# Projecting the values of four heads in one block, tokens stationary, in a two-block float32 kernel on one Trainium2 core

## What is computed

```
z_f, z_b, i, q, g = split(h @ w_in)              # w_in: 2048 x 10240; q and g for x alone
v = heads(i)                                     # 16 heads of 128
for each direction (forward, backward), each head:
    f = lb + (1 - lb) * sigmoid(z);  k = (1 - lb) * sigmoid(-z)
    b = cumsum(log f) in chunks of 64 tokens
    dS[n] = (k * exp(b_last - b))[n].T @ v[n];  S[n+1] = exp(b_last) * S[n] + dS[n]
    scores = mask((q * exp(b)) @ (k * exp(-b)).T)
    o += (q * exp(b)) @ S[n] + scores @ v
y = rms(o) * onorm_g * silu(g) @ w_out
```

## Time and profile before

| | us |
|---|---|
| median of 3 runs | 2552.0 (2551.85 to 2552.26) |
| the profiled execution | 2551.78 |
| its span | 2550.0 |
| PE busy | 2505.7 (98%) |
| DVE busy | 1648.3 (65%) |
| ACT busy | 1125.4 (44%) |

### The profile page before, as it was taken

How to read it: one execution, slowest core, us unless ns; L and a number is a source line. 1 busy time by engine, 2 the same in 40 slices (tenths; PEclk the granted TensorE clock), 3 DMA queues, 4 the chain that set the end, 5 groups by cost and what they waited for, 6 DMA issues and landing times.

```text
span 2550.0 us, 34782 instructions
## 1 busy us (share of the span) xinstructions
PE 2505.7 (98%) x13215; PEld 2059.8 (81%) x13215; DVE 1648.3 (65%) x2404; ACT 1125.4 (44%) x1923; POOL 0.2 (0%) x4
## 2 busy tenths in 40 slices
PE   6999999999999999999999999999999999999998
PEld 2578788888887888888888888878888887987887
DVE  2368789788997546464545557567566757657664
ACT  3422122222225635353534446456455646555563
POOL 0000000000000000000000000000000000000000
PEclk8999999999999999999999999999999999999999
DMA  9975376656675523333332425665544465644463
GB/s 372 375 272 171 119 214 190 201 168 214 229 247 165 151 81 103 94 99 99 94 104 82 115 83 180 203 221 176 176 154 157 162 238 183 189 159 154 165 212 134
DMA packets 380893, 440.34 MB, mean 173 GB/s; under 512 B 23086, under 2 KB 254312, under 8 KB 378856
## 3 DMA queue, kind: packets, MB, share of 16 engines
q1 hardware_dynamic: 372544, 414.24, 50.3%
q10 hardware_dynamic: 8232, 24.52, 2.6%
HBM read 430.29 MB, written 8.41 MB: 172 GB/s over the span
## 4 chain that ended last, share of the span: by engine, by line
PE 94%; DVE 2%; DMA 2%; ACT 1%; issue 1%; ACTq 0%; DVEq 0%; SPq 0%
PE ps L1280 15%; PE ps L1281 15%; PE ps L1282 15%; PE ps L1283 13%; PE ps L1285 13%; PE ps L1284 13%; PE ps L1304 1%; DMA raw<-in_ada_w_dram 1%; PE ps L1957 1%; PE ps L1965 1%; PE ps L1660 1%; PE ps L1652 1%; PE ps L1689 1%; PE ps L1664 1%; PE ps L1418 1%
## 5 line engine op out<-in xcount | busy, mean ns | idle before, releaser
L2058 DVE TENSOR_TENSOR wl<-raw,wh 128x1024 fp32r<-128x1024 f32 (+1 forms) x586 | 693.6, 1206 | 316.9 <-ACT wh L665 308.7
L665 ACT ACTIVATE wh<-raw 128x1024 fp32r<-128x1024 f32 (+1 forms) x586 | 596.6, 1043 | 624.4 <-PE ps L1285 237.7
L1280 PE MATMUL ps<-hTh,wh 128*128 128x512 f32 (+1 forms) x1820 | 681.4, 374 | 3.4 <-DVE wl L2058 1.9
L1281 PE MATMUL ps<-hTl,wh 128*128 128x512 f32 (+1 forms) x1820 | 673.8, 370 | 0.0
L1282 PE MATMUL ps<-hTh,wl 128*128 128x512 f32 (+1 forms) x1820 | 672.1, 369 | 0.0
L1283 PE MATMUL ps<-wh,hTh 128*128 128x512 f32 (+2 forms) x1568 | 614.9, 392 | 2.3 <-DVE hTl L2778 2.3
L1285 PE MATMUL ps<-wh,hTl 128*128 128x512 f32 (+2 forms) x1568 | 604.7, 386 | 0.0
L1284 PE MATMUL ps<-wl,hTh 128*128 128x512 f32 (+2 forms) x1568 | 603.7, 385 | 0.0
L1280 PEld LDWEIGHTS ps<-hTh,wh 128*128 128x128 f32 x1820 | 342.8, 188 | 71.6 <-issue 7.5
L1282 PEld LDWEIGHTS ps<-hTh,wl 128*128 128x128 f32 x1820 | 342.2, 188 | 60.0
L1281 PEld LDWEIGHTS ps<-hTl,wh 128*128 128x128 f32 x1820 | 343.0, 188 | 58.7 <-issue 1.0
(11 more groups left out here) (310 smaller groups left out, 1869.9 us busy)
## 6 DMA issues: line engine op xcount, KB each, us to landing
raw<-in_ada_w_dram SPq DMA_DIRECT2D x96, 1024.0 KB, 5.9
raw<-in_w_in_dram SPq DMA_DIRECT2D x88, 1024.0 KB, 5.2
raw<-in_od_w_in_dram SPq DMA_DIRECT2D x256, 256.0 KB, 3.8
raw<-in_ev_w_in_dram SPq DMA_DIRECT2D x192, 256.0 KB, 4.3
raw<-in_w_out_dram SPq DMA_DIRECT2D x32, 1024.0 KB, 5.1
raw<-in_ev_w_out_dram SPq DMA_DIRECT2D x16, 1024.0 KB, 5.1
raw<-in_od_w_in_dram SPq DMA_DIRECT2D x16, 1024.0 KB, 5.0
raw<-in_od_w_out_dram SPq DMA_DIRECT2D x16, 1024.0 KB, 5.1
```

The costliest lines, as they stand in the source:

```text
L665: nc.scalar.activation(wh[:, ch.spl, part], raw[:, ch.raw, part], ACT.Copy).then_inc(s_hi, 1)
L1280: nc.tensor.matmul(out, w_h, x_h, start=first, stop=False, skip_group_check=True)
L1281: nc.tensor.matmul(out, w_h, x_l, start=False, stop=False, skip_group_check=True)
L2058: nc.vector.tensor_tensor(wl[:, ch.spl, part], raw[:, ch.raw, part], wh[:, ch.spl, part].bitcast(F32), ALU.subtract).then_inc(s_lo, 1)
```

## The change

The values of four heads are projected together as a block of 512 columns, with the four token tiles stationary and the weights streaming into banks 0 to 3 (`values_project`). The result has tokens on partitions, so `v_turn`, its copy and its semaphore go. ACT moves the four banks to `V4` (`move_values`), two of them only after `keep` of the head before. A head's own chunk is now z, z, q: 384 columns for each k tile, loaded with six DMAs instead of four. The sequence of projections is `LANES`: v0, h1, h2, h3, h4, v1, h5, ... h16. The loops over heads are written out. A block of PE that computes no head (the one after a values block) has no `k_turn`, `state_scores` or `head_sum`. The splits stand one position earlier on ACT and DVE. In the entry the units are ordered anew, and four pieces of v0 run on the tokens of `x` before any on `ctx`.

```diff
+VALUE_TILE = (2, 3, 0, 1)
+LANES = [x for j in range(4) for x in [("v", j)] + [("h", 4 * j + i + 1) for i in range(4)]]
...
-            ("hg", 16, [4] * 4),
+            *((f"{kind}{i}", 1, [1] * 4 if kind == "v" else [6] * 4) for kind, i in LANES),
...
-        UNITS = [(0, 0), (0, 1), (0, 2), (1, 0), (1, 1), (1, 2)] + [(v, i) for i in range(3, 8) for v in range(2)]
+        UNITS = [(v, i) for v in range(2) for i in range(4)] + [(v, i) for i in range(4, 8) for v in range(2)]
...
-            sp.wait_ge(s_plo, KT + 3)
+            sp.wait_ge(s_plo, KT + 4)
+            sp.wait_ge(s_xq, 4)
...
+            def move_values(j):
+
+                if j:
+                    act.wait_ge(s_ds, 4 * j)
+                for bank, t in enumerate(VALUE_TILE):
+                    if bank == 2 and j:
+                        keep(4 * j)
+                        act.wait_ge(s_keep, 4 * j)
+                    nc.scalar.activation(V4[t], ps[:, bank, :], ACT.Copy).then_inc(s_v, 1)
...
+            def values_project(j, p, banks=range(4)):
+
+                ch = st.chunk(f"v{j}", 0, p // 2)
+                pe.wait_ge(s_lo, ch.half(p % 2))
+                for t in range(2):
+                    k = 2 * p + t
+                    w = slice((k % 4) * BLK, (k % 4 + 1) * BLK)
+                    for bank in banks:
+                        m = VALUE_TILE[bank]
...
+                        if j == 0 and t == 0 and m % 2 == 0:
+                            pe.wait_ge(s_plo, unit_low(m // 2, p))
+                        tok = slice(m * P, (m + 1) * P)
+                        ins = three(ps[:, bank, :], wh[:, ch.spl, w], wl[:, ch.spl, w], hTh[:, k, tok], hTl[:, k, tok], k == 0, k == KT - 1, False)
...
-            for c in range(2):
-                first_project(c, 0)
-            unit_turn(3)
+            for p in range(4):
+                values_project(0, p, (2, 3))
+                if p == 0:
+                    unit_turn(3)
             unit_turn(4)
             unit_turn(5)
...
+            for p in range(4):
+                values_project(0, p, (0, 1))
+                unit_turn(6 + 2 * p)
+                unit_turn(7 + 2 * p)
...
-                    if p == 0:
-                        v_turn(h)
-                    if p == 6:
+                    if p == 6 and h:
                         k_turn(h)
-                state_scores(h)
-                if fin:
+                if h:
+                    state_scores(h)
+                if h > 1:
                     head_sum(h - 1)
```

More of the change, by code:

```diff
@@ new lines, in move_values, with block @@
+            def move_values(j):
[6 more added lines that the diff above has]
+                    nc.scalar.activation(V4[t], ps[:, bank, :], ACT.Copy).then_inc(s_v, 1)
+            def block(b, split, extra=None):
+                h = LANES[b - 1][1] if LANES[b - 1][0] == "h" else 0
+                past = LANES[b - 2][1] if b > 1 and LANES[b - 2][0] == "h" else 0
+                split(0)
@@ L947, in log_forget @@
+                if past and h:
+                    keep(past)
+                if not h:
+                    move_values(LANES[b - 1][1])
+                split(2)
                 def log_forget(d):
@@ L998, in _ @@
             save_gates(1)
-            hi_head(1, 0)
+            hi_lane(1, 0)
+            hi_lane(1, 1)
             nc.scalar.preload_act_table_set("natural_log_exp_and_others")
@@ L1009, in _, with second @@
             act.wait_ge(s_plo, 2 * KT)
-            head(1, lambda c: head_chunks(1)(c) if c else None, fin=False, moved=lambda: spread_gates(1), between=sines)
-            head(2, head_chunks(2), fin=False)
-            with act.Fori(3, HEADS) as h, step.loop(h, 3, HEADS - 3, 6):
-                head(h, head_chunks(h))
+            def second(p):
+                if p > 1:
+                    hi_lane(1, p)
+                if p == 2:
+                    spread_gates(1)
+            block(1, second, sines)
+            for b in range(2, len(LANES)):
+                block(b, lambda p: hi_lane(b, p))
             x_rows = lambda t: x_save[t * P:(t + 1) * P, :]
@@ L1038, in gate_chunks @@
                     gate_high(p // 4 - 1)
-            head(HEADS, gate_chunks)
+            block(len(LANES), gate_chunks)
             hi(st.chunk("gate", 0, 8))
@@ L1773, in out1_chunk @@
                         ins.then_inc(s_used, 1)
-            head(HEADS, gate_chunk)
+            block(len(LANES), gate_chunk)
             gate_chunk(8)
@@ L2619, in _, with block @@
             chunked = lambda x: x.rearrange("p (n c) -> p n c", c=CHUNK)
-            def head(h, split, comp=True, fin=True, between=None):
+            def block(h, past, split, between=None):
                 def bound(x, d):
@@ L2744, in gate_chunks @@
                     gate_low(p // 4 - 1)
-            head(HEADS, gate_chunks)
+            lane_block(len(LANES), gate_chunks)
             lo(st.chunk("gate", 0, 8))
-            head(HEADS + 1, lambda p: lo(st.chunk("gate", 0, 9)), comp=False)
+            lo(st.chunk("gate", 0, 9))
+            block(0, HEADS, lambda p: None)
             gate_product(1)
```

296 lines of the change are left out of this document (146 added, 150 removed).

## The result

| | before | after |
|---|---|---|
| median of 20 runs each | 2552.18 us | 2557.57 us (2555.07 to 2559.85) |
| ratio | | 1.0017, 95% interval 1.0011 to 1.0023 |
| the profiled execution | 2551.78 | 2555.14 |
| last matmul starts at | 2542.32 | 2545.60 |

The prediction was 2554.1 with a range of 2549.0 to 2560.0; the time lies in the range. The change costs a little where it was meant to be even. The times of one kernel differ by some 2 to 5 us.

A forecast was written before the change was run, and what follows sets the result against it. PE, busy 98% of the span, was taken to bound the kernel, so time is its instructions plus its waits. The terms -7.0 + 4.6 + 3.5 + 1.0 = +2.1 on 2552.0 gave 2554.1 us, range 2549.0 to 2560.0.

The forecast's parts named there:

- The projections, 0: Recurrence layer's projections: the new k tiles of 1.74 and 2.72 us take the same total, 154.9 us per four heads.
- Rival (c): Head k tiles: the extra 0.01 us of the groups behind q goes, -5.1 us, giving 2549.0; chance 0.08.
- `v_turn`, -7.0: In the heads: removing `v_turn` saves 0.44 us on PE in each of 16 heads, 7.0 us.
- the cover of ordinary blocks: Ordinary head blocks: splits and keys still arrive in time for PE, tightest with 1.05 us to spare; 0 change.
- Four starts, +4.6: Heads 2, 6, 10 and 14: each start waits for ACT to empty bank 0, 1.15 us each, 4.6 us.
- the 0.08 for the slow first pair: At each uncovered head start: a slow first matmul pair adds 0.08 us, part of the 1.15 us.
- The entry, +3.5: Entry of the layer: PE waits 7.75 us against 3.8 before, less 0.5 for cheaper matmuls; +3.5 us.
- rival (a): Entry: the clock falls to half after the 4.8 us wait, +2.7 us, giving 2556.8; chance 0.20.
- The last block, +1.0: Last head's block: PE waits 1.0 us at gate chunk 6, its split delayed by table loads; +1.0 us.
- rival (b): Ordinary blocks: states, reciprocals and splits come too late, +7.6 us if 2 us late, giving 2561.7; chance 0.14.
- (d): Whole sum: the extra behind q goes and the entry costs nothing, -6.5 us, giving 2545.5; chance 0.05.
- (e): Last head's block: dearer table switches make split 6 and PE 4.1 us later, giving 2558.2; chance 0.03.

The follow-up runs named there:

- experiment 6: Kernel before, without the `v_turn` transposes of most heads in three versions: medians 2550.19, 2551.20, 2553.02 us; and written out with transposes kept: 2553.70.
- experiment 7: Changed kernel with the splits of every block one position later on ACT and DVE, as in the kernel before: 2590.75 us in one run.
- experiment 5: Changed kernel with forward z of heads 2, 6, 10 and 14 put in bank 3: median 2553.94 us, lowest 2551.77.
- experiment 4: Changed kernel with the splits of its last block (gate chunks) back at their old places: median 2556.05 us, lowest 2554.07.
- experiment 2: Changed kernel with 19 matmuls that nobody reads filling TensorE's long wait in the entry: median 2554.32 us, lowest 2554.14.
- experiment 1: Changed kernel run again with no edit: median 2557.36 us over 11 runs, profiled execution 2557.73.
- experiment 3: Changed kernel with only the split of the entry's fourth values piece moved earlier on ACT and DVE: median 2551.30 us, lowest 2550.35.
- experiment 8: Changed kernel with the edits of experiments 3, 4 and 5 together: median 2547.11 us, lowest 2545.37, 0.9975 of the kernel before.
- the second kernel without transposes: Kernel before without the values' transposes of heads 2 to 15, their signal given by a matmul of the next step: median 2551.20 us, lowest 2550.30.
- experiment 9: Kernel of experiment 8 with the entry's two remaining waits filled with 4 and 8 matmuls that nobody reads: median 2546.47 us, lowest 2546.22.
- the first and the third kernel without transposes: Kernel before without transposes of heads 2 to 16, waits kept: median 2550.19 us; its written-out form without those of heads 2 to 15 and their waits: 2553.02.

## Why the prediction came out as it did

- **The projections, 0**: right. 1.74 and 2.72 us a k tile, and 0.227 for a values matmul. Rival (c) falls: in a k tile of two groups and q the groups behind q are still the dearer ones.
- **`v_turn`, -7.0**: near in size in this change (the account's -2.6, less the 3.6 of the four starts, leaves -6.2), wrong in its reason. The step read the length of the row and the slow matmul behind it, and took all of it to be on the path. By itself it is worth 0.06 to 0.07 us a head (experiment 6). The working gave the other part of the change, the splits one ahead, no value, and its 0 for the cover of ordinary blocks held only because both came together (experiment 7: 33 us without it). That these two terms came out is in part luck.
- **Four starts, +4.6**: 1.15 each was foretold; 0.89 each is what goes when they go (experiment 5), 3.6 in all. Mis-sized were two parts of it. ACT began to empty the bank 0.45 after the start of the last product in the earlier trace rows, here 0.32 after it (1076.18 against 1075.86). And the 0.08 for the slow first pair is not there: from its first matmul on the head is 0.05 shorter than without the wait.
- **The entry, +3.5**: the waits are right within 0.4 us each (0.39, 4.47, 2.15 for 0.7, 4.8, 2.25), and the entry without the clock costs 5.3 - 1.6 = 3.7. (The working has 24 matmuls for a piece on `x`; it is 12, and its 2.7 us is right for 12.) The step that failed is the state of the clock, which the sum left at full speed: I gave its fall 0.20, and it fell in all five traces with the long wait (the changed kernel twice, experiments 4, 5 and 7). Its price is 1.6 us in the lower group and, by the two profiled executions, 2.3 more in the upper one, where rival (a) had 2.7 in all. That is the distance from 2554.1 to the median of 2557.57: 1.6 + 2.3, less 0.4 by which the other terms together were too dear (1.7 measured for 2.1). The time lies in the range because the range was drawn up past (a).
- **The last block, +1.0**: right, 1.09 at gate chunk 6, for the reason given; gone in experiment 4.
- **Ordinary blocks, 0**: right, PE has no wait in them, so rival (b) falls. **(d)** and **(e)** fall as well: the entry's waits are there, and a load of tables takes its 1.28.

The Trainium skill (TensorE: Matmul & The Clock Gate, Why this matters for your kernels) warned of just this, that idle time between bursts of matmuls puts the clock back. The runs agree, and experiment 2 shows that it is the idle time and not the place: same start of the piece, 3 us less.

## What to carry to other kernels

Price a removed instruction by what TensorE waits for at its end, read on the engine that delivers it, and not by its own length: a short one can hide another engine's lateness, and then its removal pays only together with an earlier delivery. Price a new wait of some microseconds by its length plus what the work behind it loses at half clock, and see first whether moving one step, or filling the wait with work that nobody reads, avoids it. When a scheme puts a projection directly behind another into the same bank, look for a bank that is idle at that time.

## What the runs showed of the hardware

- After TensorE had stood idle 4.5 us in otherwise dense work, the granted clock fell to the 1.2 GHz level in all five traces with that wait: in two within the wait (experiments 1 and 7), in three 0.2 to 0.7 us after it. Matmuls of 512 columns then stand 0.43 us apart instead of 0.23. It fell a second time at the wait of 2.15 us that follows the long one (experiments 1 and 5), and after the same wait where the one ahead was 1.20 us (experiments 3 and 8). After waits of 1.89 and 1.42 us, in the kernel before, it did not fall in the profiled execution, but it did in two of the four kernels of experiment 6.
- The kernel before is not free of it. Its written-out form (experiment 6) was profiled at 2555.20, 3.2 above its lowest run, and had its fall near the program's start, behind a wait of 1.81 us for weights that a DMA brings; the second kernel without transposes had the same, behind 1.97 us.

```profile
92.00:96.00 4.00, 4.00 (x15) 3.57 (x15) 0.51 (x3) 1.41 (x3) 0.00 (x0) 0.50 1.05 387
```

- The profiled time goes with the falls in every kernel that has more than one run. Without one after the program's first 50 us it is within 0.1 us of the kernel's lowest run (the kernel before, experiments 2 and 9). With one where the lowest runs seem to have none it is 1.5 to 2.0 above (experiments 3 and 8, the first and the third kernel without transposes). The changed kernel and the one of experiment 4 have the long wait and were profiled with one fall, 0.1 and 0.3 above their lowest runs, so there even the lowest seem to have it. With two, or one that lasts as long as two, it is 2.7 to 3.4 above (experiments 1 and 5, the other two kernels of experiment 6). A difference of 1 to 3 us between two runs of one of these kernels is thus most likely the clock at one or two places, and a median hides which. For the runs that have no trace this is not shown.
